# Mixture-of-experts weights: half blocks of the first pair in separate buffers, down blocks by column halves

## What is computed

```python
def grouped_moe(x, router_w, router_bias, w_gate, w_up, w_down):
    x2 = x.reshape(-1, d)
    aff = jax.nn.sigmoid((x2 @ router_w).astype(jnp.float32))
    ...
    def step(acc, ew):
        g_e, wg_e, wu_e, wd_e = ew
        h = jax.nn.silu(x2 @ wg_e) * (x2 @ wu_e)
        return acc + (h @ wd_e) * g_e[:, None].astype(x2.dtype), None
    out, _ = lax.scan(step, jnp.zeros_like(x2), (gates.T, w_gate, w_up, w_down))
    return out.reshape(bsz, seq, d)
...
        x = layer_norm(ALPHA * x + mix, ln_mix_g[l], ln_mix_b[l])
        ffn = grouped_moe(x, router_w, router_bias, moe_w_gate[l], moe_w_up[l], moe_w_down[l])
        x = layer_norm(ALPHA * x + ffn, ln_ffn_g[l], ln_ffn_b[l])
```

## Time and profile before

| | |
|---|---|
| device time, median of 3 runs | 1227.42 us (1223.19 to 1228.55) |
| span of the profiled execution | 1222.7 us |
| PE busy | 1149.3 us, 94% |
| mean granted TensorE clock | 0.981 of full |
| DMA traffic over the span | 321.58 MB, mean 263 GB/s |

### The profile page before, as it was taken

The page is one execution under the profiler, slowest core; times in us unless marked ns, Lnnn a source line. Parts: engine busy times, 40 slices in busy tenths (PEclk is TensorE's granted clock), DMA queues, the critical chain, the costliest instruction groups (busy, mean ns, idle before and its releaser), DMA issues.

```text
span 1222.7 us, 16385 instructions
## 1 busy us (share of the span) xinstructions
PE 1149.3 (94%) x6658; PEld 810.0 (66%) x6658; DVE 616.1 (50%) x880; ACT 457.8 (37%) x712; POOL 220.7 (18%) x194
## 2 busy tenths in 40 slices
PE   7999999999879998999999889999999988999998
PEld 6966544444339876644444336889887767998996
DVE  4787522121135878512122136884599884645544
ACT  3434412111034565412111025474565534444442
POOL 5500000000010000000000000487798541000000
PEclk9999899999999999799999999999999999999999
DMA  9489599999997336699999984452353331463550
GB/s 321 140 283 372 213 406 422 421 422 420 422 368 242 138 138 266 277 405 422 421 421 421 422 323 173 153 192 103 132 180 138 138 138 69 178 236 138 206 207 35
DMA packets 86597, 321.58 MB, mean 263 GB/s; under 512 B 7128, under 2 KB 18821, under 8 KB 61947
## 3 DMA queue, kind: packets, MB, share of 16 engines
q1 hardware_dynamic: 83776, 313.08, 66.1%
q0 software_dynamic: 2192, 7.23, 1.8%
q10 hardware_dynamic: 554, 0.22, 0.1%
HBM read 318.55 MB, written 1.96 MB: 262 GB/s over the span
## 4 chain that ended last, share of the span: by engine, by line
PE 63%; DVE 16%; DMA 9%; ACT 6%; issue 3%; POOL 1%; SPq 1%; DVEq 0%; ACTq 0%
PE bank L1641 32%; PE bank L1825 20%; DMA arena<-in_moe_w_up_dram 4%; DVE w_lo L699 2%; DMA arena<-in_moe_w_down_dram 2%; DMA ring<-in_w_kv_dram 2%; ACT w_hi L1057 2%; PE bank L1894 1%; PE bank L1721 1%; POOL w_lo L699 1%; SPq L807 1%; PE bank L1858 1%; PE bank L1816 1%; DVE rows L3026 1%; DVE arena L3045 1%
## 5 line engine op out<-in xcount | busy, mean ns | idle before, releaser
L699 POOL TENSOR_TENSOR w_lo<-ring,w_hi 128x512 fp32r<-128x512 f32 (+1 forms) x124 | 177.4, 1463 | 678.6 <-ACT w_hi L1057 678.6
L1057 ACT ACTIVATE w_hi<-ring 128x2048 fp32r<-128x2048 f32 (+1 forms) x102 | 191.9, 1884 | 196.0 <-PE bank L1641 194.3
L699 DVE TENSOR_TENSOR w_lo<-ring,w_hi 128x2048 fp32r<-128x2048 f32 x71 | 161.8, 2282 | 141.0 <-ACT w_hi L1057 141.0
L1641 PE MATMUL bank<-x_hi,w_hi 128*128 128x256 f32 x680 | 113.0, 288 | 2.4 <-issue 2.4
L1641 PE MATMUL bank<-x_hi,w_lo 128*128 128x256 f32 x680 | 110.0, 284 | 3.3 <-POOL w_lo L699 2.1
L1641 PE MATMUL bank<-x_lo,w_hi 128*128 128x256 f32 x680 | 109.7, 284 | 0.8 <-DVE x_lo L2382 0.7
L1825 PE MATMUL bank<-arena 128*64 128x512 f32 x352 | 98.6, 594 | 2.3 <-DMA arena<-in_moe_w_down_dram 1.8
L1641 PE MATMUL bank<-w_hi,x_hi 128*128 128x512 f32 x320 | 91.7, 400 | 6.8 <-DVE x_lo L2505 2.9
L1641 PEld LDWEIGHTS bank<-x_hi,w_hi 128*128 128x128 f32 x680 | 93.9, 192 | 5.2 <-issue 4.7
L1641 PEld LDWEIGHTS bank<-x_hi,w_lo 128*128 128x128 f32 x680 | 94.0, 192 | 3.9 <-POOL w_lo L699 2.5
L2683 DVE TENSOR_TENSOR y_r<-bank,y_r 128x512 fp32r<-128x512 f32 x32 | 22.1, 692 | 146.5 <-ACT y_r L1057 146.5
(11 more groups left out here) (363 smaller groups left out, 1627.7 us busy)
## 6 DMA issues: line engine op xcount, KB each, us to landing
ring<-in_w_in_dram SPq DMA_DIRECT2D x15, 2048.0 KB, 7.8
arena<-in_moe_w_gate_dram SPq DMA_DIRECT2D x24, 1024.0 KB, 15.3
ring<-in_moe_w_gate_dram SPq DMA_DIRECT2D x24, 1024.0 KB, 15.4
arena<-in_moe_w_down_dram SPq DMA_DIRECT2D x24, 1024.0 KB, 21.8
ring<-in_moe_w_down_dram SPq DMA_DIRECT2D x24, 1024.0 KB, 18.7
ring<-in_moe_w_up_dram SPq DMA_DIRECT2D x24, 1024.0 KB, 19.9
arena<-in_moe_w_up_dram SPq DMA_DIRECT2D x24, 1024.0 KB, 22.6
wslots<-in_moe_w_up_dram SPq DMA_DIRECT2D x16, 1024.0 KB, 17.6
```

Source lines behind the costliest of these rows:

```text
L699: last = ops.tensor_tensor(part(w_lo, label, hb)[:, x].bitcast(F32R), ring_half(label, hb)[:, x], part(w_hi, label, hb)[:, x], ALU.subtract)
L1057: return s.activation(dst, src, ACT.Copy)
L1641: last = mm(bank(use_)[0:still.shape[1], at:at + cols], still, moving, start=start and opens and (hb, n, k) == (0, 0, 0), stop=stop and cl ...
```

## The change

Per layer, the second halves of three blocks of the first pair, gate 0, up 0 and down 0 (`APART`), no longer go to their slots but to three other places: scratch in `arena`, `y_r` (`apart_y`) and `rows[1]` (`apart_rows`). The second half of the slot that each leaves takes at once the second half of the block that comes next in that slot: up 2, down 2 and gate 4 (`EARLY`). So eight blocks and three halves are loaded ahead of the stage, and three halves fewer within it. All six of these halves signal one semaphore, `apart_landed`, and PE waits for all six before the first gate product. Up 0's and down 0's second halves are issued behind the last of the eight blocks, and gate 0's last of all, after the experts are chosen (`chosen`), since its place is scratch of that choice.

A half of a down block is now a half of its columns: four runs of 2 KB per partition instead of one of 8 KB. A load into the first half of a slot that a down block leaves waits only for that product's first column half.

Since `rows[1]` is taken until the first down product is done, POOL waits for it before it loads the two rows of the norm behind the stage; the shift's row `mix_shift` gets a semaphore of its own.

```diff
+APART = {("gate", 0): 0, ("up", 0): 1, ("down", 0): 2}
+EARLY = {("up", 2): 0, ("down", 2): 1, ("gate", 4): 2}
...
+            if i == 1:
+                with nc.sbuf_tensor("apart_rows", [P, BLK // 2], F32) as apart_rows:
+                    pass
...
+        with nc.sbuf_tensor("below_y", [P, 2 * BLK + 2 * D], F32), nc.sbuf_tensor("apart_y", [P, BLK // 2], F32) as apart_y:
+            pass
...
+        apart = (again_(3 * BLK + 2 * NT * 2 * P + 2 * T, BLK // 2), apart_y[:], apart_rows[:])
...
-            slot_due[slot] += 32 if label[0] in ("gate", "up", "down") else 16
+            whole = label[0] in ("gate", "up", "down") and (label[0], label[2]) not in {**APART, **EARLY}
+            slot_due[slot] += 32 if whole else 16
...
+        def expert_piece(label, hb):
+            kind, l, e = label
+            if hb and (kind, e) in APART:
+                piece = apart[APART[kind, e]]
+            else:
+                piece = slots[blocks[label]["slot"]][:, hb * (BLK // 2):(hb + 1) * (BLK // 2)]
+            return piece.rearrange("p (k n) -> p k n", n=HALF)
+        def expert_landed(pe, label):
+            kind, l, e = label
+            landed(pe, label)
+            if (kind, e) in APART:
+                pe.wait_ge(sem("apart_landed"), 96 * (l + 1))
+            elif (kind, e) in EARLY:
+                pe.wait_ge(sem("apart_landed"), 96 * (l + 1))
...
             def load_half(label, hb):
-                b = blocks[label]
-                n = BLK // b["cols"] // 2
-                k = slice(hb * n, (hb + 1) * n)
-                sp.dma_start(block(label)[:, k, :], b["src"][:, k, :]).then_inc(slot_landed[b["slot"]], 16)
+                kind, l, e = label
+                src = blocks[label]["src"]
+                src = src[:, :, hb * HALF:(hb + 1) * HALF] if kind == "down" else src[:, 4 * hb:4 * hb + 4, :]
+                if hb and (kind, e) in APART:
+                    signal = sem("apart_landed")
+                elif hb and (kind, e) in EARLY:
+                    signal = sem("apart_landed")
+                else:
+                    signal = slot_landed[blocks[label]["slot"]]
+                sp.dma_start(expert_piece(label, hb), src).then_inc(signal, 16)
+            followers = {a_: b_ for a_, i in APART.items() for b_, j in EARLY.items() if i == j}
...
-                    for hb in range(2):
-                        load_half(label, hb)
+                    load_half(label, 0)
+                    kind, e = followers.get((label[0], label[2]), (label[0], label[2]))
+                    load_half((kind, l, e), 1)
+                load_half(("up", l, 0), 1)
+                load_half(("down", l, 0), 1)
+                sp.wait_ge(sem("chosen"), l + 1)
+                load_half(("gate", l, 0), 1)
                 for n in range(len(slots), len(MOE_BLOCKS), 2):
                     for hb in range(2):
                         for kind, e in MOE_BLOCKS[n:n + 2]:
+                            if hb and (kind, e) in EARLY:
+                                continue
                             before = blocks[kind, l, e]["before"]
-                            if hb == 0 and before[0][0] != "down":
+                            if hb == 0 and before[0][0] == "down":
+                                ready(sp, ("y", l, before[0][2] // 2, 0))
+                            elif hb == 0:
                                 half_read(sp, before[0])
                             else:
                                 was_read(sp, *before)
...
-                load_row(mix_shift, a["ln_mix_b"], l, "rows1")
+                load_row(mix_shift, a["ln_mix_b"], l, "mix_shift")
+                ready(pool, ("y", l, 0, 1))
                 for k, src in enumerate((a["ln_ffn_g"], a["ln_ffn_b"])):
                     load_row(rows[1][:, k, :], src, l, "rows1")
...
-                        landed(pe, (kind, l, 2 * u + half))
+                        expert_landed(pe, (kind, l, 2 * u + half))
...
-                                      lambda half, k: block((kind, l, 2 * u + half))[:, k, :],
+                                      lambda half, k: expert_piece((kind, l, 2 * u + half), k // 4)[:, k % 4, :],
...
-                        landed(pe, ("down", l, 2 * u + half))
+                        expert_landed(pe, ("down", l, 2 * u + half))
...
-                                          lambda half, j: block(("down", l, 2 * u + half))[:, j, h * HALF:(h + 1) * HALF]),
+                                          lambda half, j: expert_piece(("down", l, 2 * u + half), h)[:, j, :]),
...
-                dve.wait_ge(sem("rows1"), 48 * (l + 1))
+                dve.wait_ge(sem("mix_shift"), 16 * (l + 1))
...
-                dve.wait_ge(sem("rows1"), 48 * (int(n[2:]) // 2 + 1))
+                dve.wait_ge(sem("rows1"), 32 * (int(n[2:]) // 2 + 1))
```

## The result

| | before | after |
|---|---|---|
| device time, median | 1226.99 us (1223.19 to 1228.55, 4 runs) | 1239.61 us (1237.66 to 1242.95, 4 runs) |
| ratio | | 1.0116, 95% interval 1.0086 to 1.0146 |
| again, in a later comparison | 1223.96 us (11 runs) | 1241.78 us (6 runs), ratio 1.0143 (1.0115 to 1.0170) |
| profiled span | 1222.7 us | 1236.6 us |

The change costs 14 us by the first ratio (10.6 to 17.9) and 17.5 by the second (14.1 to 20.8), where 8.6 was forecast. (The ratio is not that of the two medians, which differ by 12.6 us in the first comparison and 17.8 in the second.) The sign was right and the size too small. The two profiled spans differ by 13.9 us.

The account below looks back on a forecast made before the run. The MoE stages were taken as bound by their saturated DMA weight stream. Terms (late start, three halves, 2 KB runs, dry spell, late rows) gave 1.8 and 6.8 us, together 8.6 later: 1236.0 us, range 1225 to 1241.

Parts of the forecast that it names:

- the late start: Start of both MoE stages: wait ahead of the first gate product plus lowered clock, 1.1 and 6.1 us.
- What bounds the kernel: Both MoE stages: the DMA stream at 421 GB/s, 2.49 us a half, sets the stage's end while PE waits there.
- Three halves ahead: Stream behind the first products: second halves of up 2, down 2 and gate 4 leave it, 7.5 us less per stage.
- The first product waits: First gate product waits for all six halves: 1.1 us later in the first stage, 4.6 in the second.
- The clock: Second stage's first product after an idle 4.6 us: lowered TensorE clock costs 1.5 us, between 0 and 1.6.
- rival C: MoE stages slower than counted: stream gaps, four clock falls at the last pairs, or 360 GB/s runs; 15 us, 1242, chance 0.08.
- Down blocks by columns: Down halves in the full stream: 2 KB runs cost 0.18 us more each, 4.9 us per stage (3.5 to 7.3).
- Release by columns, dry spell: First stage's dry queue: 2.0 us instead of 1.2, so 0.8 us more; counted for each stage.
- Rows of the norm: After down 0's product: two rows of 0.5 MB now load inside the full stream, 2.5 us more per stage.
- Rival A: Down halves in both MoE stages: 2 KB runs cost nothing, sum -1.2 us, 1226.2 us, no difference; chance 0.18.
- Rival B: Full stretch of both stages: finer runs even out engine sharing, some 430 GB/s, 1218.2 us; chance 0.07.
- D: Early loads of both stages: the halves are not ahead at all; excluded by SP's issue order, before the choice's wait.

Follow-up runs that it names:

- experiment 10: The changed kernel itself measured again on the same chip, against the kernel before: 1241.78 us against 1223.96, ratio 1.0143.
- experiment 6: Changed kernel with own signals, columns for pair 0 only, just gate 0's and up 0's halves apart, norm rows early: 1223.50 us, ratio 0.9983 to the kernel before.
- experiment 5: Changed kernel with own signals for the apart halves, gate 0's loaded first, and columns for pair 0's down blocks only: 1220.96 us, ratio 0.9965 to the kernel before.
- experiment 1: Changed kernel with only pair 0's down blocks loaded and released by columns, later ones in 8 KB runs: 1229.44 us, ratio 1.0037 to the kernel before.
- experiment 3: Kernel before with only the norm's two rows loaded late, after the first down product: 1232.34 us against 1225.63, ratio 1.0051.
- experiment 2: Kernel before with only the down blocks loaded, read and released by column halves: 1236.11 us against 1225.63, ratio 1.0089.
- experiment 7: Kernel before with each down half as eight runs of 1 KB per partition, no earlier release: 1258.05 us in a single run.
- experiment 9: Changed kernel with 1 and 4 constant matmuls ahead of the two stages' first gate product waits: 1240.06 us against 1223.96, ratio 1.0132.

## Why the prediction was right or wrong

The mechanism was right, and every term has its sign. The step that failed is the late start of the two stages, the wait ahead of the first product with the clock's fall behind it. The sum has 1.1 + 6.1 = 7.2 us for it. The profiled run has 2.5 + 5.5 + 2.76 = 10.8, and that is 3.6 of the 5.3 us that the sum is short. (In the second run, experiment 10, it is 2.8 + 4.9 + 1.77 = 9.5.) The next is the price of the 2 KB runs, 1.0 us short over both stages.

**What bounds the kernel.** Right. Each experiment that changed the stream or its start changed the in-stage times, and the last down product in after still starts on a landing in both stages (354.12 and 732.81, above). The one exception is the first stage of experiment 6.

**Three halves ahead.** Right in kind, and 7.5 us per stage fits the in-stage times to about 1 us: experiment 5's -3.3 and -3.2 us stand against -7.5 + 0.8 + 2.5 = -4.2.

**The first product waits.** The landing was worked out well: 25.55 us from the issue of the last preloaded block (488.75) to the product (514.3), 25.84 measured (494.37 to 520.21, the issue by SP's timeline of after); in the first stage 21.55, measured 21.49 (122.98 to 144.47). The queue stayed full behind the choice of experts, as assumed: 414 GB/s from 494 to 518 us. What failed is the other side of the difference, that PE would be ready when it was before. In the first stage the slots came free 1.5 us later in the profiled run, as the first eight matmuls of the product ahead took 3.6 us for 2.3 at low clock, while PE's own readiness stayed at 141.89: a wait of 2.58 us for the 1.1 forecast (1.94 in the second run of the same kernel). In the second stage PE was ready 20.4 us after that issue instead of 21.0, and waited 5.47 (4.90 in the second run) for 4.6. One trace of before gave no bound for this: over the profiled runs here the time from that issue to PE's readiness went from 18.9 to 20.5 us in the first stage, with before at 20.5, and from 18.9 to 22.2 in the second.

SP's issue of the last preloaded blocks in after, both stages, then the window of 494 to 518 us, in which the second stage's last preloads come in, and the time from issue to landing of that stage's gate 0 half (506.81 + 13.2 = 520.0, and the product starts at 520.21):

```profile
122.98 0.33 SPq L841 DMA_DIRECT2D wslots<-in_moe_w_up_dram  x1
...
133.79 0.33 SPq L841 DMA_DIRECT2D arena<-in_moe_w_gate_dram  x1
...
494.37 0.33 SPq L841 DMA_DIRECT2D wslots<-in_moe_w_up_dram  x1
...
506.81 0.34 SPq L841 DMA_DIRECT2D arena<-in_moe_w_gate_dram  x1
...
494.00:518.00 24.00, 18.74 (x102) 0.79 1.02 414
...
arena<-in_moe_w_gate_dram SPq DMA_DIRECT2D x1, 1024.0 KB, 13.2
```

**The clock.** The term was mis-sized in the second stage: 2.76 us and 1.77 in two runs for my 1.5, whose bound of 1.6 was too low. The row it came from was a pause of 3.2 us with a few matmuls in it, and the new one is 5.5 us with none. I also left out falls at the last pairs. Before has two products there at low clock for a part (8.61 us at 320.55, 8.78 at 688.18), each of the two runs of the changed kernel has three; the one at 354.12 cost 1.7 us. That was rival C's mechanism, which I priced by its count of falls and gave 0.08.

**Down blocks by columns.** Right in kind; 0.20 us a half for my 0.18, 27 x 0.20 = 5.4 for 4.9 per stage. The 512 B of the Trainium skill ("DMA: Bandwidth & Descriptors", Specifications) does not hold for this stream as a size from which the rate is full: 409 to 410 GB/s with a third of the bytes in 2 KB runs and 392 to 393 in 1 KB runs, against 421.

**Release by columns, dry spell.** Right to the accuracy of the windows: 1.2 and 2.0 us expected, 1.3 and 2.0 measured between 163 and 170 us. In experiment 1, where pair 1's down halves are in runs of 8 KB again, the same window has 280 GB/s, which is 2.3.

**Rows of the norm.** Right: 2.5 us per stage expected, 3.1 and 1.9 measured in experiment 3.

**The sum.** The last down products were forecast at 351.5 to 352 and about 727 us and start at 354.12 and 732.81. Of the 5.3 us by which the profiled difference of 13.9 exceeds 8.6, 1.0 is the runs' price (2 x 0.5), 2.3 the two waits (1.4 and 0.9) and 1.3 the second stage's fall of the clock; 0.5 lies between the stages, where the fall at 354.12 is, and the rest is rounding. The first ratio, 14 us, agrees with this bill. The second, 17.5 us, is 3.6 more, and its interval lies just above 13.9. The bill of that run (experiment 10) puts the difference behind the second stage: from the last down product to the end it has 4.5 us more than the first run. Of these 1.7 are that product itself, at low clock for a part (8.77 us for 7.09). The other 2.8 stay open. The number of low-clock products at the last pairs does not tell the two runs apart, for each has three.

**Rival A** fell with the 410 GB/s of the changed kernel and with experiments 1, 2 and 7. **Rival B** had no support: the changed kernel's full stretches are at 410 GB/s, 2.56 us a half, where it wanted less than 2.45. **Rival C** was right on the clock in part. Its gaps in the stream did not come: SP was held longer (the last section), but the share stayed at 1.02 to 1.03 at 410 GB/s. Its price for runs at 360 GB/s was wrong too: 27 halves at 0.42 us more are 11.4 us a stage, which makes the sum 21.6 and not 15. **D** was rightly excluded, for experiment 5 gains by the same halves.

## What to carry to other kernels

Where a stage lives on a saturated stream of loads, cost every edit in the stream's own time: what it moves into the stretch, in which runs, and when the stretch can begin. A preloaded byte is a gain only if the first consumer doesn't wait for it; give each transfer that is due later its own signal, and load first what is read first. Use finer releases only at the places where the queue runs dry, since finer runs are paid on every transfer.

## What the runs showed of the hardware that I had not expected

With the smaller runs SP ran less far ahead of the landings. In before an up half and a block of key weights took 27.94 and 26.15 us from issue to landing. In after the chain at the same place shows SP held for 9.19 and 8.64 us on single issues and a landing of 15.46 us. For the down halves that go to `arena` the pages give a median of 21.8 us from issue to landing before and 16.7 after. At the measured rates 27.94 us are some eleven halves in the queue and 15.46 us some six (an estimate). Whether the queue's depth goes by the number of runs, no experiment separates.

```profile
320.66 9.19 SPq L841
...
329.89 8.64 SPq L841
...
338.57 15.46 DMA arena<-in_moe_w_down_dram
```

I saw no harm from SP's blocked time, since the stream stayed full (410 GB/s), but it makes the chain of waits read as if SP were the bound.

A fall of TensorE's clock costs what it meets: 2.76, 1.77 or 1.69 us (8.78 for 7.09) at a product that others wait for, and holding it off at one place (experiment 9) moved the program's time by less than could be measured, and its profiled run has one more fall at the last pairs.
